# Last layer norm by halves, context panels of the norms in two parts, and the layer-norm update spread over the panels that follow it

## The reference, cut to what matters

```python
    m = (silu_c @ ada_w[i] + ada_b[i])[:, None, :]
    sh1, sc1, g1, sh2, sc2, g2 = jnp.split(m, 6, axis=-1)
    ...
    h_lat = layer_norm(DEEPNORM_ALPHA * h_lat + g1 * y, ln1_g[i], ln1_b[i])
    f = conv_ffn(modulate_2(h_lat, sh2, sc2), ffn_w_in[i], ffn_conv_w[i], ffn_conv_b[i], ffn_w_out[i])
    h_lat = layer_norm(DEEPNORM_ALPHA * h_lat + g2 * f, ln2_g[i], ln2_b[i])
    if need_ctx:
        h_ctx = layer_norm(DEEPNORM_ALPHA * h_ctx + cg1 * yc, ln1_g[i], ln1_b[i])
        fc = conv_ffn(modulate_2(h_ctx, csh2, csc2), ffn_w_in[i], ...)
```

## Time and profile before

| what | value |
|---|---|
| time, median of 3 runs | 4094.75 us (4091.03 to 4096.25) |
| the profiled execution, its own time | 4092.89 us |
| its span, first to last instruction | 4091.1 us |
| PE busy | 3827.3 us (94%) |
| DVE busy | 2177.4 us (53%) |
| ACT busy | 1402.8 us (34%) |
| POOL busy | 1478.4 us (36%) |
| mean granted TensorE clock | 0.966 |

### The profile page before, as it was taken

One profiled execution on the slowest core, in us unless ns is written; L12 is line 12 of the kernel. 1 busy time (PEld: TensorE's weight loads), 2 busy tenths in 40 slices (PEclk: granted clock), 3 DMA queues, 4 the chain that ended last, 5 costly groups with the idle time before them and its releaser, 6 DMA issues.

```text
span 4091.1 us, 65068 instructions
## 1 busy us (share of the span) xinstructions
PE 3827.3 (94%) x25613; PEld 3194.5 (78%) x25613; DVE 2177.4 (53%) x3518; ACT 1402.8 (34%) x1956; POOL 1478.4 (36%) x503
## 2 busy tenths in 40 slices
PE   6999989999999997899999998998999899989997
PEld 5888867888888886788886676876878888878785
DVE  6444766444644385856535445677665534433332
ACT  3322343322422233232234443242425433435231
POOL 1343322443344332234431002243447743334431
PEclk9999989999999998899999999898999999989998
DMA  5444424444444341444321001243344432212221
GB/s 179 154 152 135 150 57 134 140 150 138 152 137 156 103 125 46 130 137 150 108 76 22 13 23 63 83 128 105 126 134 144 153 107 59 77 53 89 87 90 53
DMA packets 560079, 441.64 MB, mean 108 GB/s; under 512 B 60396, under 2 KB 558077, under 8 KB 559613
## 3 DMA queue, kind: packets, MB, share of 16 engines
q1 hardware_dynamic: 559869, 438.67, 34.7%
HBM read 431.58 MB, written 2.83 MB: 106 GB/s over the span
## 4 chain that ended last, share of the span: by engine, by line
PE 66%; DVE 14%; issue 11%; ACT 4%; POOL 2%; DMA 1%; SPq 1%; DVEq 0%; ACTq 0%; POOLq 0%
PE ps_all L2199 19%; PE ps_all L2201 18%; PE ps_all L2200 18%; DVE acc L2875 4%; DMA g_raw<-in_w_mod_dram 1%; PE ps_all L1940 1%; PE ps_all L2184 1%; PE ps_all L1960 1%; ACT w_hi L1375 1%; PE ps_all L2034 1%; PE ps_all L2179 1%; DVE prod_t L2985 1%; DVE gate_t L2724 1%; PE ps_all L2180 1%; ACT prod_t L1501 1%
## 5 line engine op out<-in xcount | busy, mean ns | idle before, releaser
L872 POOL TENSOR_TENSOR w_lo<-raw,w_hi 128x2048 fp32r<-128x2048 f32 (+4 forms) x284 | 1187.1, 4181 | 2265.4 <-ACT w_hi L1375 2164.1
L2199 PE MATMUL ps_all<-h_hi,w_hi 128*128 128x512 f32 (+1 forms) x2704 | 1065.5, 394 | 22.7 <-ACT gate_t L1496 10.4
L2201 PE MATMUL ps_all<-h_hi,w_lo 128*128 128x512 f32 (+1 forms) x2704 | 1050.8, 389 | 0.0
L2200 PE MATMUL ps_all<-h_lo,w_hi 128*128 128x512 f32 (+1 forms) x2704 | 1050.4, 388 | 0.0
L1375 ACT ACTIVATE w_hi<-raw 128x2048 fp32r<-128x2048 f32 (+4 forms) x278 | 472.6, 1701 | 1443.6 <-PE ps_all L2201 1301.1
L2199 PEld LDWEIGHTS ps_all<-h_hi,w_hi 128*128 128x128 f32 x2704 | 518.3, 192 | 130.2 <-issue 12.9
L2875 DVE SCALAR_TENSOR_TENSOR acc<-g_raw,c_col,acc 128x256 f32<-128x256 f32 x1104 | 618.2, 628 | 1.7
L2201 PEld LDWEIGHTS ps_all<-h_hi,w_lo 128*128 128x128 f32 x2704 | 517.2, 191 | 104.5
L2200 PEld LDWEIGHTS ps_all<-h_lo,w_hi 128*128 128x128 f32 x2704 | 518.3, 192 | 100.5 <-issue 1.0
L2199 PE MATMUL ps_all<-hid_hi,w_hi 128*128 128x512 f32 (+1 forms) x1272 | 482.2, 379 | 22.1 <-DVE hid_lo L2988 13.7
L2201 PE MATMUL ps_all<-hid_hi,w_lo 128*128 128x512 f32 (+1 forms) x1272 | 474.1, 373 | 0.0
(11 more groups left out here) (407 smaller groups left out, 5341.1 us busy)
## 6 DMA issues: line engine op xcount, KB each, us to landing
raw<-in_w_ffn_gu_dram SPq DMA_DIRECT2D x88, 1024.0 KB, 5.0
g_raw<-in_w_mod_dram SPq DMA_DIRECT2D x72, 1024.0 KB, 5.0
raw<-in_ffn_w_in_dram SPq DMA_DIRECT2D x66, 1024.0 KB, 5.0
g_raw<-in_ada_w_dram SPq DMA_DIRECT2D x48, 1024.0 KB, 5.3
raw<-in_w_ffn_down_dram SPq DMA_DIRECT2D x32, 768.0 KB, 4.9
raw<-in_w_ffn_down_dram SPq DMA_DIRECT2D x32, 640.0 KB, 4.4
raw<-in_ffn_w_out_dram SPq DMA_DIRECT2D x24, 768.0 KB, 4.9
raw<-in_ffn_w_out_dram SPq DMA_DIRECT2D x24, 640.0 KB, 4.4
```

Source lines behind the costliest of these rows:

```text
L872: nc.gpsimd.tensor_tensor(v(w_lo), v(raw), v(w_hi).bitcast(F32), ALU.subtract).then_inc(sem["w_split_lo"], 1)
L2199: nc.tensor.matmul(o, whi, mhi, start=first, stop=False)
L2200: nc.tensor.matmul(o, whi, mlo, start=False, stop=False)
L2201: return nc.tensor.matmul(o, wlo, mhi, start=False, stop=last)
```

## The change

Six edits, all in the order or the form of the same computation:

1. The last norm and the store become one step `end_step`, by halves of 256 tokens: half means, squares summed as columns, a reciprocal of 128x2, one DVE multiply and one ACT shift per panel and half in place of two DVE operations per panel, and the rows of the first half go out before the second half is shifted. The last down panel is multiplied in two halves.
2. `ln_update` becomes one DVE operation per panel inside the iterations of the next `dn`, and ACT adds the shift.
3. The context norm inside the latent `dn`, and the latent norm inside the context `dn`, are dealt out after single panels `j` and no longer after whole iterations.
4. In the norm by halves, the first squares are summed one triple before the last panel ends, the first reciprocal is taken before the second half is added, ACT splits the next weights after the first deviation, and sums and reciprocal of the second half come one panel earlier.
5. `half_of` gives the odd gemv panel to the first iteration: 3 and 2.
6. The small vectors of the norm and `r_sb` move to other addresses.

```diff
     def half_of(gemvs, i):
-        return gemvs[i * len(gemvs) // 2:(i + 1) * len(gemvs) // 2]
+        first = (len(gemvs) + 1) // 2
+        return gemvs[first:] if i else gemvs[:first]
...
     def ln_act(st, b, act, split_hi):
             square(k)
+        deviation(0)
         split_hi(ahead(tail, 1, 1, True))
-        deviation(0)
         for n in range(2 * KD):
             high(n)
...
+            if n == KD - 2:
+                deviation(1)
             if n == KD - 1:
-                deviation(1)
                 keep(0)
...
+    def end_act(st, b, act):
...
+        for n in range(KD):
+            square(n)
+        deviation(0)
+        for n in range(KD):
+            square(KD + n)
+        for n in range(KD):
+            shifted(n)
+        deviation(1)
+        for t in range(2):
+            rows_out(t)
+        for n in range(KD, 2 * KD):
+            shifted(n)
+        rows_out(2)
+        rows_out(3)
...
+                        if update and j == 0:
+                            for c in range(2):
+                                w = ds(i * (2 * N) + c * N, N)
+                                act.wait_ge(sem["x_scaled"], update["base"]["x_scaled"] + i * 2 + c + 1)
+                                nc.scalar.activation(v[:, w], v[:, w], ACT.Identity, bias=lgb_col[:, ds(i * 2 + c, 1)]).then_inc(sem["x_kept"], 1)
                         split_hi(ahead(st, i, j, last))
+                        if inner and inner["ctx"]:
+                            for k in range(4 * i + 2 * j - 6, 4 * i + 2 * j - 4) if (1, 1) <= (i, j) <= (3, 0) else ():
+                                norm_high(inner, k)
+                        elif inner:
+                            norm_high(inner, 2 * i + j)
...
+        def end_pe(st):
...
+            for k in range(KD - 2):
+                mean_of(k, 0)
+            whi, wlo = (w_view(t, 1, tail["shapes"][1]) for t in (w_hi, w_lo))
+            for h in range(2):
+                for k in range(nk):
+                    m = [t[:, half(k, h)] for t in (hid_hi, hid_lo)]
+                    ins = triple(ps_all[:, 2 + h, 0:HT], whi[:, k, :], wlo[:, k, :], *m, k == 0, k == nk - 1)
...
+            pe.wait_ge(sem["centred"], b["centred"] + KD)
+            for k in range(KD - 1):
+                mean_of(k, 1)
+            pe.wait_ge(sem["down1"], b["down1"])
+            mean_of(KD - 1, 1).then_inc(sem["mean_summed"], 1)
+            ln_squares(st, 0)
+            ln_spread(st, 0)
+            ln_squares(st, 1)
+            ln_spread(st, 1)
...
     def ln_dve(st, b, dve, ch):
+        turn_over(0)
         add_half(1)
-        turn_over(0)
         full(0)
...
-    def ln_update(st, dve, ch):
-
-        V, b = nc.vector, st["base"]
-        dve.wait_ge(sem["r_kept"], b["r_kept"] + 2)
-        done = [ch.step(V.tensor_tensor(x[:, k * S:(k + 1) * S], x[:, k * S:(k + 1) * S], r_sb[:, :], ALU.mult)) for k in range(KD)]
-        for k in range(KD):
-            ch.wait(done[k])
-            v = x[:, k * S:(k + 1) * S]
-            V.tensor_scalar(v, v, ga_col[:, k:k + 1], gb_col[:, k:k + 1], ALU.mult, ALU.add).then_inc(sem["x_new"], 1)
-        dve.wait_ge(sem["x_new"], b["x_new"] + KD)
+    def ln_update(st, i, dve):
...
+        for c in range(2):
+            v = x[:, ds(i * (2 * S) + c * S, S)]
+            nc.vector.scalar_tensor_tensor(v, v, lga_col[:, ds(i * 2 + c, 1)], r_sb[:, :], ALU.mult, ALU.mult).then_inc(sem["x_scaled"], 1)
```

More of the change, by code:

```diff
@@ L358, in ln_step, with end_step @@
     return dict(kind="ln", tail=tail, A=A, B=B, then=then, totals=tot)
+def end_step(tail, A, B):
+    return dict(kind="end", tail=tail, A=A, B=B,
+                totals=dict(half_used=1, half_added=1, mean_summed=2, centred=2 * KD, squared=2 * KD, square_summed=2, deviation=2, r_made=2, r_spread=2,
+                            x_scaled=2 * KD, x_new=2 * KD, o_tr=4, o_out=4))
 def mods_step(need, lo, hi, plus=(), half=()):
@@ L606, in build @@
     dev_col, r_col, gs_col, ga_col = rstd[:, 0:4], rstd[:, 4:8], rstd[:, 8:8 + KD], rstd[:, 8 + KD:8 + 2 * KD]
-    bs_col, gb_col = rstd[:, 40:40 + KD], rstd[:, 48:48 + KD]
+    lgs_col, lga_col, lbs_col, lgb_col = (small[:, 128 + n * KD:128 + (n + 1) * KD] for n in range(4))
     ln_stats = ps_all[:, 5, :], ps_all[:, 7, :]
@@ L945, in one @@
                         split_lo(ahead(st, i, j, last))
-                    if context and i in (1, 2):
-                        for k in range(4 * i - 4, 4 * i):
+                        for k in range(4 * i + 2 * j - 6, 4 * i + 2 * j - 4) if context and (1, 1) <= (i, j) <= (3, 0) else ():
                             h_low(inner["base"], k, k, C, full_t[:, k % 2, 0:C], dst_of(inner))
@@ L2328, in one @@
                         ins.then_inc(sem["panel_used"], 1)
-                        if st["sums"] == "square" and last:
+                        if st["sums"] in ("square", "ln") and last:
                             break
@@ new lines, in end_dve, with add_half, centre, turn_over @@
+    def end_dve(st, b, dve, ch):
+        V = nc.vector
+        tail = st["tail"]
+        def add_half(h):
+            if h == 0:
+                dve.wait_ge(sem["half_used"], b["half_used"] + 1)
+            else:
+                dve.wait_ge(sem["panel_used"], tail["p0"] + 2 * tail["iters"])
+            v = x[:, half(KD - 1, h)]
+            V.scalar_tensor_tensor(v, ps_all[:, 2 + h, 0:HT], modc[:, tail["gate"] + KD - 1:tail["gate"] + KD], v, ALU.mult, ALU.add).then_inc(sem["down1" if h else "half_added"], 1)
+        def centre(n):
+            h, k = n // KD, n % KD
+            if k == 0:
+                dve.wait_ge(sem["mean_summed"], b["mean_summed"] + h + 1)
+                dve.wait_ge(sem["down1" if h else "half_added"], b["down1"] if h else b["half_added"] + 1)
+            v = x[:, half(k, h)]
+            V.tensor_tensor(v, v, ps_s[:, h * HT:(h + 1) * HT], ALU.subtract).then_inc(sem["centred"], 1)
+        def turn_over(h):
+            dve.wait_ge(sem["deviation"], b["deviation"] + h + 1)
+            V.reciprocal(r_col[:, 2 * h:2 * h + 2], dev_col[:, 2 * h:2 * h + 2]).then_inc(sem["r_made"], 1)
+        def scale(n):
+            h, k = n // KD, n % KD
+            if k == 0:
+                dve.wait_ge(sem["squared"], b["squared"] + (h + 1) * KD)
+                dve.wait_ge(sem["centred"], b["centred"] + (h + 1) * KD)
+                dve.wait_ge(sem["r_spread"], b["r_spread"] + h + 1)
+            v = x[:, half(k, h)]
+            V.scalar_tensor_tensor(v, v, colv[:, st["A"] + k:st["A"] + k + 1], ln_stats[h][:, 0:HT], ALU.mult, ALU.mult).then_inc(sem["x_scaled"], 1)
+        add_half(0)
+        for n in range(KD):
+            centre(n)
+        add_half(1)
+        for n in range(KD, 2 * KD):
+            centre(n)
+        turn_over(0)
+        for n in range(KD):
+            scale(n)
+        turn_over(1)
+        for n in range(KD, 2 * KD):
+            scale(n)
@@ L3042, in _ @@
                 for j in range(2):
-                    dve.wait_ge(sem[f"down{j}"], b[f"down{j}"] + st["iters"] - (1 if st["sums"] == "square" and j else 0))
+                    dve.wait_ge(sem[f"down{j}"], b[f"down{j}"] + st["iters"] - (1 if st["sums"] in ("square", "ln") and j else 0))
             elif kind == "proj":
```

159 lines of the change are left out of this document (93 added, 66 removed).

## The result

The changed kernel takes 4070.07 us (median of 5 runs, 4061.70 to 4074.79) against 4091.68 us (4084.08 to 4096.25) of the kernel before beside it: 21.6 us less, ratio 0.9944 with a 95% interval of 0.9931 to 0.9957. The interval leaves out 1, so the change makes the kernel faster by 0.4 to 0.7%.

The account below looks back on a forecast made before the run. TensorE was taken to bound the kernel, busy 3827.3 of 4091.1 us, so only its stops counted. Terms -8.3 - 2.6 + 3.8 - 1.4 - 1.5 + 0 - 10 = -20.0 gave 4074.8, stated as 4074, range 4063 to 4086.

Parts of the forecast that it names:

- A: First latent down projection of block 2, edits 2 and 3: shorter PE stops for gemv sums, -8.3 us.
- D: Output projection of block 2, layer 0, edit 5: stop of 2.05 goes, that of 2.30 grows slightly, -1.4 us.
- G: The end of the kernel, edit 1: last norm and store by halves shorten the closing chain, -10 us.
- B: Two norms by halves, edit 4: stops ahead of either half's first matmuls mostly go, -1.3 each, -2.6 us.
- F: Context down projection, edit 3: same operations dealt out in another order, 0 us, unknown +-3.
- With an earlier start DVE runs alone a little longer and still meets both: Step in A: gemv panel still meets two `w_lo` runs, so the first stop falls by 6.2, from 13.4 to 7.2.
- The second stop: In A, PE's second wait for a gemv sum, 6.8 us: was to fall by 5.2, leaving 1.6.
- C: Output projection of block 1, layer 1, edit 5: new stop of about 10 us at the second sum, net +3.8.
- E: First down projection of layer 1, edit 2: PE's wait of 1.48 behind the update block goes, -1.5 us.
- the bound of -6: Smaller-gain bound of G: ACT, with squares, shifts and copies, is serial where DVE helped, about 4 more.
- The slower rival: In A and F, a chain from gemv panel to `w_lo` holds up three iterations, +30 us, 4104; chance 0.05.
- The deep case: C costs nothing, A gives 12 and F gains 2: 4065 us; chance 0.12.

Follow-up runs that it names:

- e2: Changed kernel with edit 2 undone (update of x again one block of 16 operations ahead of the first gemv panel): 12 us slower than the changed kernel.
- e3: Changed kernel with edit 3 undone (norms inside the down projections again after whole iterations): 2.6 us slower by the medians, not told from nothing.
- e4: Changed kernel with edit 4 undone (old order in both norms by halves): first norm 3.2 us shorter, second 1.3 more; no whole time given.
- f3: As f2, with edit 4 also undone in the first norm by halves alone: 2.8 us below f2, 35 us below the kernel before.
- e7: Changed kernel with POOL's w_lo cut to 8 columns of each chunk in stretches C and A: 25 us faster than the changed kernel.
- e5: Changed kernel with edit 1 undone (last norm for all tokens at once, separate store): medians differ by 6.0 us, the end 8.0 longer.
- e6: Changed kernel with another order at the end (ACT's squares and shift earlier, two row copies on DVE): medians differ by 2.1 us, the end 3.3 shorter.
- f2: Changed kernel with the alterations of e8 and e6 together: 7.6 us below the changed kernel run again on the same chip.
- e8: Changed kernel with edit 5 only where the projection carries the context, old share in block 1 layer 1: 4.7 us faster than the changed kernel.

## Why the prediction held, step by step

The sum was -20.0. The touched columns of before and after give -(-3.9 + 5.3 + 12.8 + 1.5 + 1.7 + 8.2) = -25.6, the two comparisons of medians -21.6 and -24.8. The terms for A and for D with its norm were too small and those for G and B too large, and part of that cancelled; that the time came out within 4 us is in part luck.

- **A, -8.3 predicted, -12.8 with F.** The mechanism was right (e2: 10.1 of it hangs on edit 2), the size of the first step was off. "With an earlier start DVE runs alone a little longer and still meets both" is the step that failed: the stop fell by 10.6 (13.44 to 2.88), not 6.2, since the second `w_lo` came after the gemv panel. Of the 10.6, 7.2 are the earlier start, as predicted, and 3.3 the meeting that is gone (12.08 to 8.82). The second stop fell by 6.05 (5.2 predicted), and the one that comes back at the fourth panel is 5.21, not 3.1: that panel takes 9.87, beside a `w_lo` of the next step, which has 2048 columns and takes 4.6 alone where 3.5 had been put. The reason given for the second stop, the norm dealt out, was wrong beside edit 2 (e3). The stops fell by 11.4 in all, and the granted clock rose from 0.84 (2789.3 to 2876.8 before) to 0.93 (2795 to 2870).
- **B, -2.6.** -1.5 in the second norm (e4: 1.3), -1.3 predicted. In the first the sign was wrong once edit 5 was in: the stops of 1.2 went as predicted, but edit 4 costs 1 to 3 there (e4, f3). The step that failed is pricing an order by its stops alone, with the clock of the work put at no change.
- **C, +3.8.** The columns give +3.9; the four kernels with the old share there say 2.4 to 5.5. The first stop was to stay at 3.1 and is 3.19, the new one was to be about 10 and is 9.43, the later ones 4.5 and are 4.2; the two meetings are as described, and e7 shows that they are the cause.
- **D, -1.4.** With the first norm -5.3, where -2.7 was predicted. The two stops came out as described (2.46 and 0.25), 1.6 less in all. By themselves the edits don't add up there: both undone +5.3, edit 5 alone undone +1.4, edit 4 alone undone -3.2, so that without edit 4 edit 5 would be worth 8.5. The clock takes part in this (0.79 over 2580 to 2645 before), and with a scatter of 2 us how much each has of it stays open.
- **E, -1.5**: -1.7 (e2: 2.6). **F, 0**: not to be told from nothing.
- **G, -10**: -8.2, e5 8.0. The chain from the last means on was to be 31 and is 31.7. The second squares cost 5.79 for 4.26 but began at 10.0 behind that point for 11.1, so they ended at 15.8 where 15.4 was put; the last copy ended at 28.3 for 27.3. The other part is PE's stop of 0.69 ahead of the last means, which was put at nothing. ACT's order was only in the bound of -6; another one is worth 2 to 3.3 (e6, f2, f3).
- **The slower rival** did not come: in A PE never waits for `w_lo`. But DVE does hold POOL up there (6.76 for 3.5), the first half of that chain. The deep case is what e8 and f2 reach: C without its cost.

The Trainium skill (SBUF — State Buffer, section "Who interferes with whom") says that whoever issues first gets the shared ports for the whole instruction and the other fully blocks. The traces agree, operation by operation: one DVE operation stands 3.65 us beside a `w_lo` of 3.5 in the kernel before, one 3.56 in the changed kernel, and in e7 POOL stands in its turn, 3.71 for an operation of 0.4 to 0.7. What the prediction drew from that sentence was too short: DVE's hold on POOL outlasts a single operation, since POOL got in only behind eight of them at 2794 and at once at 2795.43 in the kernel before. The prediction also told the section's rule on one SBUF input without its condition: it holds outside the modes that use two ports, and `tensor_scalar` is named there as one that can enter them. The stop of such an operation, told in the last section below, agrees with that.

## What to carry to other kernels

When DVE work with two SBUF operands runs beside POOL work, cost it by how many POOL operations it meets, and ask when those become ready; an earlier start may meet fewer. A second cure for the same wait can be worth nothing beside the first (edit 3: 2.9 us of stops alone, none beside edit 2): measure edits to one stall one at a time and together. Count stops in the same matmuls and not in the same microseconds, since a kernel that runs late takes a stop out of the window. Where an edit takes stops out of PE, look at the granted clock of the stretch before booking the gain: in A the work itself became 5.0 us shorter (e7), in the first norm it became 4.5 longer (the changed kernel against e4).

## What was not expected of the hardware

An operation with one SBUF operand stands too, which the prediction left out. In the changed kernel's output projection of block 2 the pair of first products takes 4.97 us beside a `w_lo`, against 0.62 alone (above, at 1659.25); DVE and POOL:

```profile
2567.72 4.97 DVE L3000 TENSOR_SCALAR acc<-g_raw,c_col 128x256 f32<-128x256 f32 x2
```

```profile
2567.67 4.61 POOL L879 TENSOR_TENSOR w_lo<-raw,w_hi 128x2048 fp32r<-128x2048 f32 x1 [8.35 <-ACT w_hi L1422]
```

The pair began 0.05 us after POOL and lost nearly its time (4.35 of 4.61); the 14 multiply-adds behind it took 5.75. The kernel before has the same in that projection (4.96 at 2556.43). And POOL's share is large: cutting `w_lo` in two of the kernel's stretches gave back 25 us, more than the whole change. That kernel leaves out most of the low parts of these weights, so it tells what the meetings cost and is no kernel to use.
